# Probabilities times values in two column halves of TensorE, and a transpose back for each head group

## What is computed

```python
p = jnp.exp(s - m)
p = p / (jnp.sum(p, -1, keepdims=True) + ...)          # the sink's term in group A only
o = jnp.einsum('bnhgqk,bnkhd->bnqhgd', p.astype(v.dtype), vb)
```

## Time and profile before

| | |
|---|---|
| runs | 1011.61 us median of 3 (1010.88 to 1014.06) |
| profiled execution | span 1005.1 us from the first to the last instruction |
| TensorE busy (matmuls) | 919.4 us, 91% |
| VectorE, ScalarE, GpSimd busy | 61%, 53%, 18% |
| mean granted TensorE clock | 0.956 |
| attention stage, first and second sequence | about 44 to 218 us and 296 to 462 us of the span |

### The profile page before, as it was taken

How to read it: one execution, slowest core, us unless ns; L and a number is a source line. 1 busy time by engine, 2 the same in 40 slices (tenths; PEclk the granted TensorE clock), 3 DMA queues, 4 the chain that set the end, 5 groups by cost and what they waited for, 6 DMA issues and landing times.

```text
span 1005.1 us, 15974 instructions
## 1 busy us (share of the span) xinstructions
PE 919.4 (91%) x4959; PEld 744.9 (74%) x4960; DVE 616.7 (61%) x1182; ACT 534.2 (53%) x1008; POOL 177.8 (18%) x260
## 2 busy tenths in 40 slices
PE   5899999899989999989973999999999999999982
PEld 5777888687877788867742788888888888888850
DVE  5443644655744573465698989989456494564684
ACT  4343565542445565554343878877446584464460
POOL 4300002001000011100011234435222232221301
PEclk9998999989999999989975999999999999999996
DMA  8740114116342352310755999999868697674524
GB/s 252 120 108 22 42 43 130 61 43 201 115 104 84 112 183 54 116 42 22 281 215 171 352 362 394 389 374 392 275 203 260 197 342 228 218 248 116 150 107 193
DMA packets 95119, 183.95 MB, mean 183 GB/s; under 512 B 24064, under 2 KB 52975, under 8 KB 95072
## 3 DMA queue, kind: packets, MB, share of 16 engines
q1 hardware_dynamic: 80496, 137.91, 38.3%
q0 software_dynamic: 14144, 43.88, 16.4%
q10 hardware_dynamic: 432, 1.57, 0.4%
HBM read 159.85 MB, written 28.70 MB: 188 GB/s over the span
## 4 chain that ended last, share of the span: by engine, by line
PE 41%; DVE 15%; issue 6%; DMA 4%; ACT 3%; DVEq 1%; SPq 0%; ACTq 0%; POOL 0%; POOLq 0%
PE O L2009 9%; PE C L1728 7%; PE C L1730 7%; PE C L1729 7%; DVE split_main L1594 6%; PE O L1909 3%; PE T L1962 2%; PE S L1763 2%; PE T L1884 2%; PE S L1969 1%; PE T L1792 1%; DMA mixing<-in_w_out 1%; DMA mixing<-acc_dram 1%; ACT split_main L1092 1%; DVE mixing L1675 1%
## 5 line engine op out<-in xcount | busy, mean ns | idle before, releaser
L1594 DVE TENSOR_TENSOR split_main<-mixing,split_main 128x1024 fp32r<-128x1024 f32 x188 | 217.7, 1221 | 35.0 <-ACT split_main L1092 32.3
L1092 ACT CAST split_main<-mixing 128x1024 fp32r<-128x1024 f32 x188 | 186.4, 1050 | 17.2 <-PE C L1730 7.1
L1728 PE MATMUL C<-split_main,split_aux 128*128 128x512 f32 x368 | 143.9, 391 | 1.3 <-DVE split_aux L1600 1.3
L1730 PE MATMUL C<-split_main,split_aux 128*128 128x512 f32 x368 | 143.9, 391 | 0.0
L1729 PE MATMUL C<-split_main,split_aux 128*128 128x512 f32 x368 | 143.6, 390 | 0.0
L1728 PE MATMUL C<-split_main 128*128 128x512 f32 (+1 forms) x320 | 130.4, 407 | 3.5 <-DVE split_main L1434 3.0
L2009 PE MATMUL O<-split_main,split_aux 128*128 128x512 f32 x552 | 132.7, 396 | 0.0
L1729 PE MATMUL C<-split_main 128*128 128x512 f32 (+1 forms) x320 | 121.6, 380 | 0.0
L1730 PE MATMUL C<-split_main 128*128 128x512 f32 (+1 forms) x320 | 121.4, 379 | 0.0
L2009 PEld LDWEIGHTS O<-split_main,split_aux 128*128 128x128 f32 x552 | 100.2, 188 | 23.4 <-DVE split_aux L1615 4.7
L1728 PEld LDWEIGHTS C<-split_main,split_aux 128*128 128x128 f32 x368 | 69.5, 189 | 15.9 <-issue 1.5
(11 more groups left out here) (341 smaller groups left out, 1435.3 us busy)
## 6 DMA issues: line engine op xcount, KB each, us to landing
mixing<-in_w_down SPq DMA_DIRECT2D x64, 512.0 KB, 8.2
mixing<-in_w_gate SPq DMA_DIRECT2D x64, 512.0 KB, 9.1
mixing<-in_w_up SPq DMA_DIRECT2D x64, 512.0 KB, 6.1
mixing<-in_w_in SPq DMA_DIRECT2D x20, 512.0 KB, 3.8
mixing<-in_w_out SPq DMA_DIRECT2D x16, 512.0 KB, 4.1
mixing<-in_w_mem_kv SPq DMA_DIRECT2D x8, 512.0 KB, 6.1
mixing<-in_w_in SPq DMA_DIRECT2D x16, 256.0 KB, 3.7
x_dram<-x_nat POOLq DMA_DIRECT2D x8, 512.0 KB, 2.9
```

The lines of the kernel that those rows point to most:

```text
L1092: nc.scalar.copy(wu[0][:, w, :], raw[:, w, :]).then_inc(unit_hi, 1)
L1594: nc.vector.tensor_tensor(wu[1][:, w, :], raw[:, w, :], wu[0][:, w, :].bitcast(F32), ALU.subtract).then_inc(unit_lo, 1)
L1728: ins = nc.tensor.matmul(out_ap, st[0], mvg[0], start=first, stop=False)
L1730: ins = nc.tensor.matmul(out_ap, st[1], mvg[0], start=False, stop=last)
```

## The change

The event `PV` now stands for a pair, not for a unit. The value rows (128 keys x 64 columns) are the stationary operand and the transposed probabilities (128 columns) the moving one. The first head's result goes to partitions 0 to 63 of the bank and the second's to 64 to 127, so the two heads lie in two column halves of the array; the matmuls alternate between the heads. The result has its head columns on the partitions and the queries along the free axis. Two new events turn it back for each group: `OC`, where ScalarE copies the 128x512 bank into `o_sb`, and `OT`, where TensorE transposes the four 128x128 blocks into a bank of the `Tb` ring. `G` multiplies from that bank. `OC` stands between `T` and `S`, `OT` and `G` behind the pieces of the projections; behind the loop `OC` and `OT` lie on both sides of `W` for tile 3 and `G` stays where it was.

```diff
+            group = (p - 5) // 4 if p >= 5 and p % 4 == 1 else None
+            if group is not None:
+                ev.append(("OC", s, group))
             if p < NP:
                 ev.append(("S", s, p))
-            if p >= 5 and p % 4 == 1:
-                ev.append(("G", s, (p - 5) // 4))
             for t in range(2):
                 if nxt < 48 and nxt < (p + 1) * 12 // 7:
                     piece(s, 6 + nxt // 4, nxt % 4)
                     nxt += 1
+            if group is not None:
+                t_unit("OT", s, group)
+                ev.append(("G", s, group))
...
             if p >= 1:
-                for i in (2 * p - 2, 2 * p - 1):
-                    ev.append(("PV", s, i, s * NU + i))
+                ev.append(("PV", s, p - 1))
+        ev.append(("OC", s, NGR - 1))
         wo(s, 0, 0, (3,), True)
+        t_unit("OT", s, NGR - 1)
         wo(s, 0, 1, (0, 1))
         ev.append(("G", s, NGR - 1))
...
+                elif what == "OC":
+                    gi = s * NGR + ev[2]
+                    act.wait_ge(pv_done, (gi + 1) * GU)
...
+                    nc.scalar.copy(turn_cols(ev[2]), Ob[gi % 2][:, :].rearrange("p (n c) -> p n c", n=NT)).then_inc(o_copied[gi % 2], 1)
...
-                    dve.wait_ge(pv_done, a + 1)
...
-                    nc.vector.tensor_tensor(dst, Ob[gi % 2][:, :].rearrange("p (n e d) -> p n e d", n=NT, e=2),
+                    u = T_OF_OUT[gi]
+                    dve.wait_ge(t_ready[u % 2], u // 2 + 1)
+                    nc.vector.tensor_tensor(group_cols(gl), Tb[u % 2][:, :].rearrange("p (n e d) -> p n e d", n=NT, e=2),
                                             rden[:, gi % 2, :].rearrange("p (n e) -> p n e", e=2).unsqueeze(3)
-                                            .to_broadcast([P, NT, 2, HD]), ALU.mult).then_inc(o_drained[gi % 2], 1)
+                                            .to_broadcast([P, NT, 2, HD]), ALU.mult).then_inc(t_drained[u % 2], 1)
...
+                    for k in range(n_keys):
+                        for e in range(2):
...
+                            ins = nc.tensor.matmul(Ob[gi % 2][e * HD:(e + 1) * HD, tile * P:(tile + 1) * P], v,
+                                                   probsT[:, e, k * P:(k + 1) * P], start=(k == 0), stop=(k == n_keys - 1))
...
+                elif what == "OT":
+                    gi, u = s * NGR + ev[2], ev[3]
+                    pe.wait_ge(t_drained[u % 2], u // 2)
+                    pe.wait_ge(o_copied[gi % 2], gi // 2 + 1)
+                    for n in range(NT):
+                        ins = nc.tensor.transpose(Tb[u % 2][:, n * P:(n + 1) * P], turn_cols(ev[2])[:, n, :], ident[:, :])
+                    ins.then_inc(t_ready[u % 2], 1)
```

More of the change, by code:

```diff
@@ L258 @@
 T_OF_MIXED = {(e[0], e[1], e[2]): e[3] for e in EVENTS if e[0] in ("oA", "oM", "oB")}
+T_OF_OUT = {e[1] * NGR + e[2]: e[3] for e in EVENTS if e[0] == "OT"}
 T_OF_Q = {(e[1], e[2]): e[3] for e in EVENTS if e[0] == "Q"}
@@ L443, in build_kernel @@
         pv_done = sem("pv_done")
-        o_drained = [sem("o_drained0"), sem("o_drained1")]
+        o_copied = [sem("o_copied0"), sem("o_copied1")]
         sink_in = sem("sink_in")
@@ L565, in t_waits, with turn_cols, out_read, group_cols @@
                 eng.wait_ge(t_drained[b], (last_unit - b) // 2 + 1)
+        def turn_cols(gl):
+            kind, g = GROUPS[gl]
+            c0 = OCOL["B"] if kind == "A" else OCOL[kind] + g * P
+            return o_sb[:, :, c0:c0 + P]
+        def out_read(eng, gi):
+            u = T_OF_OUT[gi]
+            eng.wait_ge(t_ready[u % 2], u // 2 + 1)
+        def group_cols(gl):
+            kind, g = GROUPS[gl]
+            if kind == "A":
+                return o_sb[:, :, 0:A_Q].rearrange("p n (e a d) -> p n e a d", e=2, a=4)[:, :, :, g, :]
+            c0 = OCOL[kind] + g * P
+            return o_sb[:, :, c0:c0 + P].rearrange("p n (e d) -> p n e d", e=2)
+        def out_turned(eng, gi):
+            u = T_OF_OUT[gi]
+            eng.wait_ge(t_drained[u % 2], u // 2 + 1)
         def c_waits(eng, cu):
@@ L625, in group_stats @@
                 if k_ == kind and (kind != "B" or g_ == part):
-                    gi = s * NGR + gl
-                    dve.wait_ge(o_drained[gi % 2], gi // 2 + 1)
+                    out_turned(dve, s * NGR + gl)
             row = stats[:, NT + n, :, :]
@@ L1098, in exp_unit @@
                 if j == 0 and gi >= 2:
-                    act.wait_ge(o_drained[gi % 2], gi // 2)
+                    out_turned(act, gi - 2)
                 pr = probs[:, a % 2, :]
@@ L1174, in _ @@
                     copy_probs(act, nc.scalar.copy, s, i, a, u)
+                elif what == "OC":
+                    gi = s * NGR + ev[2]
+                    act.wait_ge(pv_done, (gi + 1) * GU)
+                    if gi == 0:
+                        act.wait_ge(pads_stored, 16)
+                    if ev[2] in (3, 4, 5, 6):
+                        out_read(act, gi - 1)
+                    nc.scalar.copy(turn_cols(ev[2]), Ob[gi % 2][:, :].rearrange("p (n c) -> p n c", n=NT))                        .then_inc(o_copied[gi % 2], 1)
                 elif what == "NM":
@@ L1503, in _ @@
                     gi, a = s * NGR + gl, s * NU + (gl + 1) * GU - 1
-                    if gi == 0:
-                        dve.wait_ge(pads_stored, 16)
                     den = sums[:, gi % 2, :]
@@ L1849, in _ @@
                         if pi == 0 and t == 2:
-                            pe.wait_ge(o_drained[0], (s + 1) * NGR // 2)
+                            pe.wait_ge(o_copied[0], (s + 1) * NGR // 2)
                         if pi == 0 and t == 3:
@@ L1860, in _ @@
                         if t == 1:
-                            pe.wait_ge(o_drained[1], (s + 1) * NGR // 2)
+                            pe.wait_ge(o_copied[1], (s + 1) * NGR // 2)
                         if t >= 2:
@@ L1887, in _ @@
                 elif what == "PV":
[L1888 to L1892, removed]
+                    pair = ev[2]
+                    kind, tile, h = UNIT_LIST[2 * pair]
+                    gi, j = place(s, 2 * pair)
+                    for i in (2 * pair, 2 * pair + 1):
+                        u = T_OF_UNIT[s * NU + i]
+                        pe.wait_ge(t_drained[u % 2], u // 2 + 1)
                     if j == 0 and gi >= 2:
-                        pe.wait_ge(o_drained[gi % 2], gi // 2)
+                        pe.wait_ge(o_copied[gi % 2], gi // 2)
+                    n_keys = key_range(tile)[1] // P if kind == "A" else 2
                     if kind == "M":
@@ L1897, in _ @@
                             t_waits(pe, T_OF_VALUES[(s, "mv", h // 2)])
-                        vs = [mv[:, k, h * HD:(h + 1) * HD] for k in range(2)]
                     elif kind == "A":
@@ L1901, in _ @@
                             t_waits(pe, T_OF_VALUES[(s, "va", 0)])
[L1902 to L1911, removed]
+                    elif j == 0:
+                        pe.wait_ge(vbw_loaded, 16 * (s + 1))
+                    for k in range(n_keys):
+                        for e in range(2):
+                            if kind == "M":
+                                v = mv[:, k, (h + e) * HD:(h + e + 1) * HD]
+                            elif kind == "A":
+                                v = va[:, key_range(tile)[0] // P + k, e * HD:(e + 1) * HD]
+                            else:
+                                v = vbw[:, 2 * tile + k, (h + e) * HD:(h + e + 1) * HD]
+                            ins = nc.tensor.matmul(Ob[gi % 2][e * HD:(e + 1) * HD, tile * P:(tile + 1) * P], v,
+                                                   probsT[:, e, k * P:(k + 1) * P], start=(k == 0), stop=(k == n_keys - 1))
+                            if k == n_keys - 1:
+                                ins.then_inc(pv_done, 1)
+                elif what == "OT":
[5 more added lines that the diff above has]
+                    ins.then_inc(t_ready[u % 2], 1)
                 elif what == "Q":
```

## The result

The changed kernel takes 1027.05 us (median of 4 runs, 1025.86 to 1034.33) against 1011.25 us: 1.0179 of the time before, 95% interval 1.0139 to 1.0218. The medians differ by 15.8 us, and the ratio's interval is worth 14 to 22 us; 1031 was forecast, in a range of 1014 to 1041. The span of the profiled execution grew from 1005.1 to 1024.2 us.

A forecast was written before the change was run, and what follows sets the result against it. TensorE's queue was taken to bound the attention stage. Halves -9.9, turning back +7.0, waits +17.0 and clock +5.2 gave +19.3 us on the 1011.6 median: 1031 us, range 1014 to 1041 (1022 to 1040 for the forecast alone).

The forecast's parts named there:

- The product in halves: Attention's value products: pairs with two key blocks take 0.74 us, with three 0.96; gain 9.9 us.
- the row of the four quarters: Router's f32 product in four column quarters, used as nearest price: 0.71 us, 4 rounds of 0.11 plus 0.27 for emptying.
- serial loads: Rival at the pairs: next loads not hidden, 0.91 and 1.23 us a pair, 1043.5 us; 0.08 together with no overlap.
- no overlap: Rival at the pairs: column halves do not overlap at all, 18.2 us lost, 1059 us; 0.08 together with serial loads.
- free switching: Rival at each of 64 pairs: switching the array costs nothing, gain 29.1 us, 1006.5 us; chance 0.08.
- Turning back: 16 groups of four TensorE transposes, 0.44 us a group, 7.0 us; ScalarE's copies cost nothing in the loop.
- The hold: TensorE's second transposing unit waits for VectorE's late product to empty its ring bank: iterations 9, 13, 25, 1.3 to 3.2 us.
- The wait behind the loop: After each attention loop, last product starts 1.7 us later, delaying the weight split TensorE awaits: 1.4 us more.
- Iteration 29: Late in the attention loop: hold of about 0.5 us, plus about 0.2 us waiting for ScalarE's copy.
- Iteration 5: Early in the attention loop, where the blocked unit follows sooner: a hold of about 0.3 us.
- The rival that VectorE is in time: Moved product finds VectorE free everywhere: +1.5 us, 1013 us, no measurable change; chance 0.09.
- The clock: After three of four long holds TensorE runs 3.5 us at half speed: 5.2 us charged, bounds 0 and 14.

The follow-up runs named there:

- run 1: Kernel before with only the value product changed to column halves, a pair as one event, nothing turned back; 1.0089 of before, attention stage 7.0 us shorter.
- run 2: Changed kernel, but the four transposes back go into the group's own bank instead of the `Tb` ring; 1.0026 of before, stage 473.6 us.

## Why the prediction was right

**What bounds it.** TensorE's queue, but not to the full amount that the prediction gives it. It says that a shorter queue comes back in full and a wait is paid in full. In run 1 TensorE's busy time fell by 11.5 us and the stage by 7.0; in run 2 13.8 us of waits went and the idle time fell by 8.7. Part of each went into waits for ScalarE and VectorE.

**The product in halves.** Forecast 0.74 and 0.96 us a pair, with entering and leaving. Measured: 0.10 to enter, 0.59 or 0.80 to the next transposes, and 0.05 more for those. Four transposes behind a full-array product take 0.54 us up to the scores (before), behind one in halves 0.59 (run 2):

```profile
182.02 0.61 PE L1884 MATMUL T<-ident,probs 128*128 128x128 f32 x4
182.56 0.63 PE L1763 MATMUL S<-split_main 64*128 64x256 f32 x6
```

```profile
181.07 0.66 PE L1913 MATMUL T<-ident,probs 128*128 128x128 f32 x4
181.66 0.39 PE L1792 MATMUL S<-split_main 64*128 64x256 f32 x2
```

So 0.74 and 0.95: the row of the four quarters carried over. Two more rounds cost 0.80 - 0.59 = 0.21 us, 0.11 each. What one matmul of a round needs alone is read from the bias tables of the kernel before, also f32, with 512 moving columns:

```profile
78.37 1.88 PE L1809 MATMUL T<-mixing,anti 128*128 128x512 f32 x4
80.08 1.00 PE L1909 MATMUL O<-mv,probsT 128*128 128x64 f32 x8
```

Four of them take 1.71 us, so 128 columns take about 0.11. Two such matmuls fit into one round of 0.11: the halves overlap, and the next loads are hidden. The Trainium skill, "TensorE: Matmul & The Clock Gate", section "What overlaps and what doesn't", lets weight loads overlap only between different row groups; here two column halves of one row group overlap as well, so the measurement decides against the rule for this case. The rivals built on serial loads and on no overlap fall. So does the one of free switching: about 0.30 us is paid in each stretch (0.74 less four rounds of 0.11). The gain over the stage, however, was 7.0 in run 1, not 9.9: it was lost to waits, which the sum had not charged.

**Turning back.** The four transposes of a group take 121.84 - 121.31 = 0.53 us, of which 0.10 is the entry into the halves behind them: 0.43, as forecast. That run 2's stage is 6.7 us longer than run 1's is no second measurement of the 7.0: it holds 3.4 us more idle time and 10 us less at half clock.

**The hold.** Forecast for the two sequences 1.3 + 2.6 + 3.2 and 0.95 + 2.6 + 3.2 us, 13.8 in all with nothing regained; measured 6.9 + 6.9. The wait behind the loop grew by 1.4 us, as forecast. Iteration 29 was put at 0.5 and 0.2 for the copy; no more than 0.3 us shows, in the second sequence alone. Iteration 5 was put at 0.3, which the sum leaves out; nothing shows there. The 8.4 of the second sequence would be 8.25 by its own terms. The rival that VectorE is in time is refuted by these rows.

**The clock.** Three of the four long holds were charged with a stretch at half clock. Busy by stretch in the profile after, behind each of the four:

```profile
125.50:128.90 3.40, 3.40 (x27) 2.44 (x27) 1.16 (x4) 1.79 (x5) 0.00 (x0) 1.00 0.53 151
185.60:188.90 3.30, 3.30 (x13) 2.36 (x13) 3.13 (x10) 1.47 (x5) 0.00 (x0) 0.50 0.45 159
380.10:383.40 3.30, 3.30 (x12) 2.32 (x13) 1.16 (x4) 1.08 (x3) 0.00 (x0) 0.50 0.55 159
441.60:444.90 3.30, 3.26 (x12) 2.45 (x13) 3.13 (x9) 1.29 (x5) 0.00 (x0) 0.50 0.45 156
```

The last column but two is the granted clock: after the holds at 182, 377 and 438 us TensorE ran at 1.2 GHz while all but fully busy, and behind the first it kept 2.4. That it was three is luck: the hold behind which the clock stayed and the one at 377 us were both 2.52 us long, and no row said which would be followed by a stretch at half clock. So is the size of 3.5 us, read from a window of the earlier trace rows: the half clock there lasted from 196.7 to 206.9 us. Over the whole stage the half clock grew by 10 us, which costs the 5.2 us that were charged, but not by these three stretches alone: the 6.8 us at 91 us of the kernel before are gone after, there is a new one at 302 us, and the one at 455 us is longer.

**The sum.** 19.3 us was forecast; 15.8 came in the medians, 18.1 by the ratio (0.0179 x 1011.25), and 16.9 in the stage. The profile's span, 19.1 us longer, agrees better than it should: 2.5 us of it lie behind the last expert product, 35.0 us after and 32.5 before, where nothing was changed. There the clock stood at half for the last 26.3 us after, and for 19.9 before. In the stage TensorE's idle time grew from 27.9 to 44.5 us, 16.6 where 17.0 of waits were forecast, and its busy time by 0.2 where 2.3 were (-9.9 + 7.0 + 5.2). The agreement is partly luck. The gain was 2.9 us smaller than priced, and nearly as much came back unforeseen: against run 1 the changed kernel has 2.4 us less of waits for L1140's exponentials, 1.0 less for the chunks' parts and 0.7 less for the copies of the probabilities, presumably since the holds give ScalarE and VectorE time. Of these 4.1 us the sum had 1.2. Iteration 29, and in the second sequence another wait for the weight split that shrank by 0.8 us, are the rest as far as it can be told.

## What to carry to other kernels

A new user of a shared ring of buffers is priced by the moment at which it empties its buffer, that is by everything that stands in front of it on the emptying engine, and the ring's next writer is where the price is paid. Operands exchanged for column halves gain only what their rounds save over entering and leaving (here about 0.3 us a stretch), so they pay for long products and not for short ones. Where a result must be turned back, look for a buffer that is free anyway, here the one just copied out, and do it only where the product is long enough.

## What was not expected

With the turning left out, the kernel became slower although its attention stage was faster: its output decides how many tiles the experts get, 48 instead of 46, about 9 us each. A variant whose values are wrong can be compared in this kernel only up to the routing.

Moving the weight split behind the loop out of the way gave 0.6 us a sequence instead of 1.4 or more: a wait of 0.75 us appeared and one of 0.71 grew to 1.02. More than one consumer hangs on the last group's product, and TensorE meets whichever is late.
